# Matmul operands moved by a few words in SBUF: other distances modulo 512 bytes between the moving and the stationary tile

## The reference, cut to what matters

```python
def peer_ffn(h, wq, sub_keys, u, v):          # per block of 128 tokens
    q = (xb @ wq).reshape(PEER_BLOCK, PEER_HEADS, 2, PEER_HALF)
    s = jnp.einsum('thpd,hpnd->thpn', q, sub_keys)
    ...                                       # top 16 of 128, top 16 of 256 sums, softmax g
    act = jax.nn.gelu(jnp.einsum('td,ted->te', xb, u[eid]))
    return jnp.einsum('te,ted->td', g * act, v[eid])

def _swiglu(h, w_gate_up, w_down):
    gu = h @ w_gate_up
    gate, up = gu[..., :D_FF], gu[..., D_FF:]
    return (jax.nn.silu(gate) * up) @ w_down
```

## Time and profile before

| | before |
|---|---|
| median of 3 runs | 2841.38 us (2837.03 to 2846.93) |
| the profiled execution, first to last instruction | 2841.9 us |
| PE busy | 2768.2 us (97%), 19552 matmuls |
| DVE, ACT, POOL busy | 2048.3, 1454.4, 179.7 us |
| granted TensorE clock | 0.990 of 2.4 GHz |
| DMA | 546.19 MB, mean 192 GB/s |

### The profile page before, as it was taken

One profiled execution on the slowest core, in us unless ns is written; L12 is line 12 of the kernel. 1 busy time (PEld: TensorE's weight loads), 2 busy tenths in 40 slices (PEclk: granted clock), 3 DMA queues, 4 the chain that ended last, 5 costly groups with the idle time before them and its releaser, 6 DMA issues.

```text
span 2841.9 us, 57248 instructions
## 1 busy us (share of the span) xinstructions
PE 2768.2 (97%) x19552; PEld 2600.4 (92%) x19552; DVE 2048.3 (72%) x4430; ACT 1454.4 (51%) x2378; POOL 179.7 (6%) x141
## 2 busy tenths in 40 slices
PE   7999999999999999989999999999999999999998
PEld 7999899999988888979999999988888889999998
DVE  8657987886567677876698888566677876666665
ACT  5455445444455555555544444455555565446444
POOL 0004000000000000000275000000000000000000
PEclk9999999999999999999999999999999999999999
DMA  5445565455766665424456554676666525553454
GB/s 191 177 152 180 202 221 203 170 180 191 239 247 242 241 242 187 148 82 156 151 179 217 184 181 168 211 251 242 244 241 240 190 90 178 188 217 125 173 190 178
DMA packets 140452, 546.19 MB, mean 192 GB/s; under 512 B 15785, under 2 KB 81593, under 8 KB 83617
## 3 DMA queue, kind: packets, MB, share of 16 engines
q1 hardware_dynamic: 63216, 455.38, 44.4%
q10 hardware_dynamic: 73728, 67.14, 7.6%
q0 software_dynamic: 3376, 21.88, 2.0%
HBM read 505.53 MB, written 40.91 MB: 192 GB/s over the span
## 4 chain that ended last, share of the span: by engine, by line
PE 80%; DVE 12%; DMA 3%; ACT 2%; issue 2%; POOL 2%; SPq 0%; DVEq 0%; ACTq 0%
PE bank L796 24%; PE bank L797 23%; PE bank L798 23%; PE bank L1016 4%; DVE wL L551 3%; DMA ring<-in_w_stream 2%; POOL wL L551 2%; PE bank L917 1%; PE bank L937 1%; ACT wH L540 1%; PE bank L928 1%; DVE pr_m L1973 0%; DVE pr_eq L1969 0%; DVE pr_eq L1971 0%; PE bank L893 0%
## 5 line engine op out<-in xcount | busy, mean ns | idle before, releaser
L551 DVE TENSOR_TENSOR wL<-ring,wH 128x1024 fp32r<-128x1024 f32 x809 | 988.3, 1224 | 632.9 <-ACT wH L540 623.0
L540 ACT ACTIVATE wH<-ring 128x1024 fp32r<-128x1024 f32 x864 | 907.4, 1055 | 407.4 <-DMA ring<-in_w_stream 230.2
L796 PE MATMUL bank<-hnH,wH 128*128 128x256 f32 x3528 | 1020.0, 289 | 21.4 <-DVE wL L551 14.6
L797 PE MATMUL bank<-hnL,wH 128*128 128x256 f32 x3528 | 1002.4, 284 | 0.0
L798 PE MATMUL bank<-hnH,wL 128*128 128x256 f32 x3528 | 1002.3, 284 | 0.0
L796 PEld LDWEIGHTS bank<-hnH,wH 128*128 128x128 f32 x3528 | 680.8, 193 | 30.4 <-issue 15.1
L797 PEld LDWEIGHTS bank<-hnL,wH 128*128 128x128 f32 x3528 | 681.2, 193 | 0.5 <-issue 0.2
L798 PEld LDWEIGHTS bank<-hnH,wL 128*128 128x128 f32 x3528 | 680.4, 193 | 0.0
L796 PE MATMUL bank<-wH,wgtH 128*128 128x512 f32 x1024 | 398.5, 389 | 0.0
L797 PE MATMUL bank<-wL,wgtH 128*128 128x512 f32 x1024 | 398.4, 389 | 0.0
L798 PE MATMUL bank<-wH,wgtL 128*128 128x512 f32 x1024 | 398.3, 389 | 0.0
(11 more groups left out here) (411 smaller groups left out, 3530.6 us busy)
## 6 DMA issues: line engine op xcount, KB each, us to landing
ring<-in_w_stream SPq DMA_DIRECT2D x432, 1024.0 KB, 4.9
act_parked<-act_out ACTq DMA_DIRECT2D x256, 128.0 KB, 2.6
act_in<-act_parked ACTq DMA_DIRECT2D x256, 128.0 KB, 2.8
sw_bias<-in_c_swa POOLq DMA_DIRECT2D x1, 4096.0 KB, 15.5
relb_rows<-rel_table POOLq DMA_DIRECT2D x1, 2048.0 KB, 9.7
h_parked<-h POOLq DMA_DIRECT2D x2, 1024.0 KB, 5.9
h_back<-h_parked POOLq DMA_DIRECT2D x2, 1024.0 KB, 6.2
od_relb<-relb_rows POOLq DMA_DIRECT2D x2, 1024.0 KB, 7.6
```

The source lines that it names most:

```text
L540: eng.activation(wH[:, b % NBUF, :], raw(b), ACT.Copy).then_inc(w_high, 1)
L551: eng.tensor_tensor(wL[:, b % NBUF, :], raw(b), wH[:, b % NBUF, :].bitcast(F32), ALU.subtract).then_inc(w_low, 1)
L796: pe.matmul(dst, lh, rh, start=start, stop=False, skip_group_check=True)
L797: pe.matmul(dst, lh, rl, start=False, stop=False, skip_group_check=True)
```

## The change

Tiles are shifted: by padding in the lists, and by allocating the small tables `small` (96 words) and `snk` (16 words) earlier, around `hn`. No instruction is added, removed or reordered. Distances are those of the moving tile from the stationary tile, in bytes modulo 512, worked out from the sizes in the lists.

| moving tile, stationary tile | distance before | after |
|---|---|---|
| `hn`, `w` and `pr_h`, `w` | 0 | 448 (64 short of 512) |
| `ff_a`, `w` | 0 | 384 |
| `mem`, `w` | 0 | 192 |
| `att_OT`, `w` | 64 | 128 |
| `od_h`, `w` | 64 | 256 |
| `od_y`, `w` | 64 | 320 |
| `ycat`, `w` | 288 | 64 |
| `w`, `wgt` and `w`, `pr_q` (weights moving) | 0 | 448 |
| `w`, `mem` | 0 | 320 |
| `w`, `hn` | 0 | 64 |

```diff
-        MEM0, ATT0 = AR - 2 * DC * T, AR - 2 * DC * T - 9344
+        MEM0, ATT0 = AR - 2 * DC * T - 96, AR - 2 * DC * T - 9344
...
-                ("poolL", [4, 256], F32R), ("ycatH", [8, 256], F32R), ("ycatL", [8, 256], F32R),
+                ("poolL", [4, 256], F32R), ("ycat_before", [56], F32), ("ycatH", [8, 256], F32R), ("ycatL", [8, 256], F32R),
...
-        _, pr_hH, pr_hL = stage(("pr_h_before", [8192], F32), ("pr_hH", [DC, T], F32R), ("pr_hL", [DC, T], F32R))
-        _, od_hH, od_hL = stage(("od_h_before", [8720], F32), ("od_hH", [DC, T], F32R), ("od_hL", [DC, T], F32R))
-        _, od_rels = stage(("od_rels_before", [12816], F32), ("od_rels", [16, T], F32))
+        _, pr_hH, pr_hL = stage(("pr_h_before", [8288], F32), ("pr_hH", [DC, T], F32R), ("pr_hL", [DC, T], F32R))
+        _, od_hH, od_hL = stage(("od_h_before", [8752], F32), ("od_hH", [DC, T], F32R), ("od_hL", [DC, T], F32R))
+        _, od_rels = stage(("od_rels_before", [12864], F32), ("od_rels", [16, T], F32))
...
-                ("od_iw", [2, 8], F32), ("od_sel", [2, 256], F32),
+                ("od_iw", [2, 8], F32), ("od_between", [48], F32), ("od_sel", [2, 256], F32),
...
-        ff_s, ff_f, ff_g, ff_u, ff_aH, ff_aL = stage(
+        ff_s, ff_f, ff_g, ff_u, _, ff_aH, ff_aL = stage(
...
-            ("ff_aH", [FC, 256], F32R), ("ff_aL", [FC, 256], F32R))
+            ("ff_between", [80], F32), ("ff_aH", [FC, 256], F32R), ("ff_aL", [FC, 256], F32R))
...
         sb("shared", [P, DC * T])
 
+        small = sb("small", [P, 96])
         hnH, hnL = sb("hnH", [P, DC, T], F32R), sb("hnL", [P, DC, T], F32R)
+        snk = sb("snk", [P, 16])
         ring = sb("ring", [P, SLOTS, 2 * BLK])
         wH, wL = sb("wH", [P, NBUF, BLK], F32R), sb("wL", [P, NBUF, BLK], F32R)
...
-        snk = sb("snk", [P, 16])
...
-        small = sb("small", [P, 96])
```

More of the change, by code:

```diff
@@ L366, in build_stacks @@
             ("att_OTL", [8, 256], F32R))
-        ev_pv, ev_u, ev_c, ev_b, ev_cu, ev_z, ev_s0, ev_s1, ev_s2, ev_s3, ev_pool, ev_cnt, ycat, poolH, poolL, \
+        ev_pv, ev_u, ev_c, ev_b, ev_cu, ev_z, ev_s0, ev_s1, ev_s2, ev_s3, ev_pool, ev_cnt, ycat, poolH, poolL, _, \
             ycatH, ycatL, mem_raw = stage(
@@ L384, in build_stacks @@
         pr_raw = pr_eq[:, 0:PEER_RAW * T].rearrange("p (a b) -> p a b", a=PEER_RAW)
-        _, pr_hH, pr_hL = stage(("pr_h_before", [8192], F32), ("pr_hH", [DC, T], F32R), ("pr_hL", [DC, T], F32R))
-        _, od_hH, od_hL = stage(("od_h_before", [8720], F32), ("od_hH", [DC, T], F32R), ("od_hL", [DC, T], F32R))
-        _, od_rels = stage(("od_rels_before", [12816], F32), ("od_rels", [16, T], F32))
+        _, pr_hH, pr_hL = stage(("pr_h_before", [8288], F32), ("pr_hH", [DC, T], F32R), ("pr_hL", [DC, T], F32R))
+        _, od_hH, od_hL = stage(("od_h_before", [8752], F32), ("od_hH", [DC, T], F32R), ("od_hL", [DC, T], F32R))
+        _, od_rels = stage(("od_rels_before", [12864], F32), ("od_rels", [16, T], F32))
         pr_tv, pr_px, pr_pa, pr_pb, pr_paf, pr_pbf = [pr_m[:, k] for k in range(6)]
         pr_e, pr_g, pr_i1, pr_i2 = [[pr_m[:, 6 + 2 * k], pr_m[:, 7 + 2 * k]] for k in range(4)]
-        od_q, od_ckv, od_ik, od_iq, od_hq, od_hf, od_hg, od_hi, od_ckvn, od_ckvT, od_iw, od_sel, od_relb, \
+        od_q, od_ckv, od_ik, od_iq, od_hq, od_hf, od_hg, od_hi, od_ckvn, od_ckvT, od_iw, _, od_sel, od_relb, \
             od_yH, od_yL, od_neg, od_rel, od_sc, hg_A, hg_f, hg_QL0, hg_QL1, hg_KL0, hg_KL1, hg_dq, hg_dk, \
```

## The result

The changed kernel takes 2850.04 us (median of 20 runs, 2840.13 to 2857.16) against 2842.18 us before (20 runs): ratio 1.0025, interval 1.0016 to 1.0034. It is slower by a quarter of a per cent, outside the noise; the prediction was 2830 us and faster.

The account below looks back on a forecast made before the run. The prediction took PE's rate of starting matmuls as the bound. Minus 25 (short), plus 13.4 (long) and plus 0.2 (`ycat`) gave minus 11 us, so 2830 us, range 2800 to 2856.

Parts of the forecast that it names:

- What bounds the kernel: All stages: PE's matmul starts set the time, so a sooner start shortens the run by nearly all it saves.
- Short matmuls at 448: `hn`, `ff_a`, `mem`, `pr_h` leaving distance 0, 12168 matmuls: 120.0 ns becomes 117.8, minus 25 us.
- The sign named for this term: PE timeline of the new kernel: `hn` steps at 117 to 118 ns with weight loads of 188 ns would confirm it.
- Long matmuls: Weights over `wgt`, `mem` and `hn` leaving distance 0, 3360 matmuls: 4 ns slower each, plus 13.4 us.
- a shift ends a pattern: At distance 0, matmul and weight load repeat a pattern costing 13.3 ns; breaking it helps short matmuls, harms long ones.
- The tiles that changed between non-zero distances: `ycat` from 288 to 64: plus 0.2 us; `att_OT`, `od_h`, `od_y`: taken as 0, between minus 1.3 and plus 2.6.
- Addresses of everything else: `ring`, weights, `con`, `vec`, `small` at new addresses: costed at nothing, hidden by PE's lead.
- The reading that the clock is granted in full in every slice: Whole profile before the change: the PE clock was read as granted in full in every slice.
- No change: Rival, chance 0.17: stage and neighbours, not distance, set the step of the matmuls; 2841 us.
- Short ones gain and long ones keep their pattern: Rival, chance 0.27: short matmuls gain, long ones keep their pattern or gain; minus 25 us, about 2816 us.
- The slower rival: Rival, chance 0.18: short matmuls gain less than 1.5 ns while long ones lose 5.3; plus 17.8 us, 2859 us.
- the forecast's mechanism: Whole kernel: short matmuls faster, long ones slower, by their new distances; about 2830 us, chance 0.36.

Follow-up runs that it names:

- experiment three: Only the short matmuls (`hn`, `ff_a`, `mem`, `pr_h`) moved to 448, weights over `wgt` left at 0, against the kernel before: 2817.94 us, ratio 0.9907.
- Half splits: ACT and DVE make only the left half of `wH` and `wL` after four blocks: 2741.68 us with short matmuls at 448, 2792.75 on the kernel before.
- half a stream: SP loads only each pair's first block after the first two pairs: 2798.3 us with short matmuls at 448, 2829.24 us on the kernel before.
- experiment one: All tiles, ring and weights included, moved 448 bytes later with distances kept, against the kernel before: 2842.91 against 2843.78 us, ratio 0.9998.
- experiment twelve: The changed kernel with ACT and DVE making only the left half of `wH` and `wL` after four blocks: 2789.07 us against its control's 2792.75.

## Why the prediction was wrong

**What bounds the kernel: wrong, and this is the step that failed.** The text said that a matmul that starts sooner shortens the run by nearly all that it saves, in every stage. The growth of the waits stood in the sum at nothing. In `outs`, `acts` and `tokens` the step holds: the waits grew by 0.6 us there. Elsewhere it doesn't: of the 24.4 us that PE waited for `wL` the prediction made a sign of slack, while it was the visible tip of a supply that just kept pace. With the short matmuls faster, idle time rose by 21 us, in the changed kernel and in experiment three alike, and by 2.5 us, within what traces differ by, when only the long ones moved. Half splits take most of that rise away, half a stream a quarter to a half. The prediction showed windows only for the two stages of the expert layer, and they say nothing about the projections, gate and up groups and norms, where ACT and DVE also have to evacuate banks. Windows of the kernel before in those stages:

```profile
330.00:500.00 170.00, 165.78 (x1368) 163.35 (x1367) 143.50 (x285) 82.02 (x129) 0.00 (x0) 1.00 0.60 208
...
1500.00:1640.00 140.00, 137.74 (x1156) 137.16 (x1156) 114.74 (x284) 68.44 (x109) 27.54 (x11) 1.00 0.59 204
...
2231.00:2480.00 249.00, 240.84 (x1892) 232.78 (x1891) 182.97 (x381) 133.24 (x265) 6.71 (x7) 0.99 0.44 160
...
2645.00:2785.00 140.00, 140.00 (x1169) 140.00 (x1169) 90.98 (x140) 67.92 (x98) 0.00 (x0) 1.00 0.51 181
```

In the first three PE is idle for 4.2, 2.3 and 8.2 us. In the last it is busy throughout, and yet the changed kernel waits 2.4 us more there. So a full window doesn't show slack either; how long a block lies ready before PE takes it does.

**The terms of the sum.** Short matmuls at 448: the step of 117.8 ns was right (117.8), the term was undersized. It was minus 25 us and is minus 34.6, since about a quarter of the unbroken `hn` steps ran near 113.3 ns, which no long stretch of the trace before had shown. The sign named for this term came too: the weight load beside `hn` takes 188 ns in the median where it took 192. Long matmuls: right in direction, undersized in price. That a shift ends a pattern is not shown: 228.9 and 233.3 ns are steady steps too. The term was plus 13.4 us; the step went to 233.3 ns, above the bound of 232 that I took from the first steps of the stage, and cost 20.4 us. The two errors nearly cancel, which was luck: the sum of the prediction was minus 11 us, the steps without waits give minus 13.2. The tiles that changed between non-zero distances came to well under 2 us, within their bounds. Addresses of everything else cost nothing, as said (experiment one). The reading that the clock is granted in full in every slice was wrong (the mean is 0.990, and the digits show only 90% or more); it entered no term.

**The rivals.** No change: refuted. The step of the same instructions moves between 116.7, 117.8 and 120.0 ns with the distance alone, while moving all tiles together changes nothing. The Trainium skill's page "SBUF — State Buffer", section "SBUF: two separate sides", says that PE never waits on anyone; what the prediction drew from it for this rival, that the distance can't matter, doesn't hold here. Whether the longer step is a wait at a port, no run shows. Short ones gain and long ones keep their pattern: experiment three shows that kernel, but the change isn't it. The slower rival had the right sign for the wrong reason: it wanted the short ones to gain less than 1.5 ns, and they gained 2.8 on average. The time lay inside the range, 2800 to 2856, and the change of a quarter of a per cent inside the 0.3% to which the prediction gave 0.23; neither came by the forecast's mechanism.

**What stays open.** Why distance matters at all, and what makes a stretch at a distance of 64 or 192 modulo 256 run at 113.3 or at 117.8 ns, wasn't settled; that it varies between executions of one program is shown. Where exactly in the order of ACT's and DVE's work the late blocks are held up was read at one place (the table load in the down product), and a kernel without that load wasn't tried. Each kernel has one trace, so differences of a few us between traces decide nothing by themselves.

## What to carry to other kernels

A stream of matmuls with a weight load each can gain or lose 2 to 6% by the distance between its moving and its stationary tile, and the best place differs by shape: here 448 was the best place tried for 256 columns and 0 for 512 columns, so the two have to be placed separately. The kernel with only the short ones moved is the best that kept the whole computation, 2817.94 us, ratio 0.9907 (2824.64 in the one run of its repetition). Before costing a faster PE, look at every stage for how late the next weight block is ready; where PE already waits for it now and then, a part of the saving is lost there, here more than half by the traces (28.2 of 49.6 us in experiment three).

## What the runs showed of the hardware that was not expected

- The step of a 256-column matmul by distance modulo 256 bytes: 0 gives 120.0 ns (seen at 0 and 256), 64 and 192 give 117.8 or 113.3 ns (seen at 64, 192, 320, 448), 128 gives 118.7 or 120.0 (at 128, 384; 120.0 for the gated activations in experiment twelve), 32 gives 116.7 or 117.8 (at 32, 288), 96 gives 120.0, 160 gives 120.0 or 118.7 (at 416), 224 gives 118.3.
- The step of a 512-column matmul: 226.7 ns at 0, 228.9 at 64 and 320, 233.3 at 32, 96 and 448.
- After a wait of PE of 3.04 us the granted clock stood at 0.51 for 3.4 us; at the same place in the kernel before, after a wait of 1.43 us, it stood at 1.00.
- One and the same stretch of one program ran at 117.7 ns in one execution and at 113.4 ns in another, with the clock granted in full.
